# Expert stage: gated rows turned inside the next slot's first product, w2 split and y copies moved one step

## The reference, cut to what matters

```python
t = x.reshape(-1, D)                       # 1088 tokens, D = 1024
# top-1 group of 4, top-2 experts of its 4  ->  gates (1088, 16)
for e in range(16):                        # w1, w3: (1024, 256), w2: (256, 1024)
    he = jax.nn.silu(t @ w1[e]) * (t @ w3[e])
    y = y + gates[:, e:e + 1] * (he @ w2[e])
```

## Time and profile before

| | us |
|---|---|
| median of 3 timed runs | 1383.54 (1375.72 to 1384.65) |
| the profiled execution | 1374.35 |
| its span, first to last instruction | 1372.5 |
| mean granted TensorE clock | 0.91 of full |
| PE busy | 1166.7 (85%) |
| DVE busy | 710.0 (52%) |
| ACT busy | 505.1 (37%) |
| POOL busy | 312.5 (23%) |

### The profile page before, as it was taken

One profiled execution on the slowest core, in us unless ns is written; L12 is line 12 of the kernel. 1 busy time (PEld: TensorE's weight loads), 2 busy tenths in 40 slices (PEclk: granted clock), 3 DMA queues, 4 the chain that ended last, 5 costly groups with the idle time before them and its releaser, 6 DMA issues.

```text
span 1372.5 us, 17867 instructions
## 1 busy us (share of the span) xinstructions
PE 1166.7 (85%) x5729; PEld 897.7 (65%) x5729; DVE 710.0 (52%) x1310; ACT 505.1 (37%) x909; POOL 312.5 (23%) x273
## 2 busy tenths in 40 slices
PE   4999999898988989999899998963898988989920
PEld 3898799835757657575758585733676767767710
DVE  4320410255545445453546463425787878778737
ACT  3334122132112112121313131301777777777712
POOL 2101300000000000000000000001666656666646
PEclk9999999999696998878999999985999999999965
DMA  6340141270001101010101010003769786764278
GB/s 235 105 143 7 56 131 45 77 219 24 16 26 55 64 16 62 16 62 16 62 17 62 16 47 8 31 31 112 239 225 344 233 279 239 253 232 170 92 264 302
DMA packets 92946, 158.90 MB, mean 116 GB/s; under 512 B 12673, under 2 KB 61265, under 8 KB 92881
## 3 DMA queue, kind: packets, MB, share of 16 engines
q1 hardware_dynamic: 80112, 113.48, 24.5%
q0 software_dynamic: 11680, 42.47, 8.8%
q10 hardware_dynamic: 1088, 2.10, 0.4%
HBM read 167.80 MB, written 40.55 MB: 152 GB/s over the span
## 4 chain that ended last, share of the span: by engine, by line
PE 59%; DVE 10%; DMA 10%; issue 9%; ACT 7%; SPq 2%; POOL 2%; POOLq 1%; ACTq 0%; DVEq 0%
PE ps L896 9%; DMA below<-in_w 6%; PE ps L863 5%; PE ps L751 5%; PE ps L733 5%; DVE low L1564 3%; PE ps L1887 3%; PE ps L1889 3%; PE ps L1888 3%; PE ps L822 3%; PE ps L1882 2%; PE ps L1881 2%; PE ps L1883 2%; ACT high L1292 2%; SPq L1185 2%
## 5 line engine op out<-in xcount | busy, mean ns | idle before, releaser
L1564 DVE TENSOR_TENSOR low<-below,high 128x1024 fp32r<-128x1024 f32 x128 | 195.8, 1576 | 70.5 <-ACT high L1292 60.9
L1745 POOL TENSOR_SCALAR arena<-arena 128x1 f32<-128x1 f32 (+5 forms) x38 | 15.8, 417 | 747.6 <-ACT arena L691 366.9
L1253 POOL TENSOR_TENSOR low<-below,high 128x1024 fp32r<-128x1024 f32 x64 | 148.5, 2338 | 103.3 <-ACT high L1313 103.3
L1389 PE MATMUL ps<-high 128*128 128x512 f32 x384 | 156.0, 406 | 16.8 <-DVE low L1574 12.5
L538 ACT ACTIVATE arena<-ps 128x512 f32<-128x512 f32 (+7 forms) x109 | 56.9, 530 | 283.1 <-PE ps L733 282.8
L1391 PE MATMUL ps<-high,low 128*128 128x512 f32 x384 | 151.0, 393 | 0.0
L1390 PE MATMUL ps<-low,high 128*128 128x512 f32 x384 | 150.8, 393 | 0.0
L1292 ACT ACTIVATE high<-below 128x1024 fp32r<-128x1024 f32 x128 | 129.1, 1052 | 50.0 <-DMA below<-in_w 50.0
L896 PE MATMUL ps<-arena 128*128 128x512 f32 (+1 forms) x288 | 125.7, 594 | 2.9 <-ACT arena L538 2.4
L733 PE MATMUL ps<-arena 128*128 128x128 f32 (+4 forms) x613 | 104.3, 299 | 12.5 <-DVE arena L1093 4.8
L733 PEld LDWEIGHTS ps<-arena 128*128 128x128 f32 (+4 forms) x613 | 81.4, 165 | 31.2 <-issue 15.0
(11 more groups left out here) (214 smaller groups left out, 2036.2 us busy)
## 6 DMA issues: line engine op xcount, KB each, us to landing
below<-in_w SPq DMA_DIRECT2D x256, 256.0 KB
below<-in_w POOLq DMA_DIRECT2D x64, 512.0 KB
y_dram<-arena SPq DMA_DIRECT2D x32, 512.0 KB, 2.8
arena<-in_x_prompt SPq DMA_DIRECT2D x16, 512.0 KB
below<-in_w_in SPq DMA_DIRECT2D x12, 512.0 KB, 7.0
out<-arena SPq DMA_DIRECT2D x9, 512.0 KB, 5.3
arena<-in_w_o SPq DMA_DIRECT2D x1, 4096.0 KB, 16.5
h_dram<-arena SPq DMA_DIRECT2D x8, 512.0 KB, 2.6
```

Of the source, the lines that this page charges most:

```text
L1253: pool.tensor_tensor(w2_lo[s % UN][:, c], w2_in[:, c], w2_hi[s % UN][:, c].bitcast(F32), ALU.subtract).then_inc(s_w2lo, 1)
L1389: pe.matmul(out, x_hi, w_hi, start=start, stop=False)
L1564: dve.tensor_tensor(chunk(w13_lo[j], c), chunk(w13_in, c), chunk(w13_hi[j], c).bitcast(F32), ALU.subtract).then_inc(s_w13lo, 1)
```

## The change

PE: the two transposes of the gated rows of slot s-1 move from the end of body s-1 to the middle of the first product of slot s, before its fifth chunk (`gated_turn`). ACT and DVE take the high and low part there (`gated_high`, `gated_low`), between chunks of the next slot's w13 split, which is itself cut in pieces: chunks (0, 1) and (2, 3) on ACT, (0), (1, 2) and (3) on DVE, the last behind the gate product and the turned tokens. The y copies of slot s-2 stand at the start of body s. ACT casts w2 of slot s at the end of body s, where it cast that of slot s+1. POOL's low parts of w2 follow, and each w2 load is issued behind the split of its chunk.

ACT, one step in the steady part of the stage. Before: silu (L1327) of slot s, high parts of the turned tokens of s+1 (L1300), y copy of s-1 (L1305), g_hi of s (L1339), w2 of s+1 (L1313), w13 of s+2 (L1292).

The diff, cut to its core:

```diff
@@ -1235,25 +1235,26 @@
                 out=xg[:, s % UN, :], out_offset=None, in_=hn_dram,
                 in_offset=bass.IndirectOffsetOnAxis(ap=tok_i[:, s:s + 1], axis=0)).then_inc(s_xg[s % UN], 16)
 
-        def load_second(s):
-            e, new = expert(pool, s)
-            for c in range(2):
-                if s:
-                    pool.wait_ge(s_w2lo, 2 * s + c - 1)
-                pool.dma_start(w2_in[:, c], w2[0, bass.ds(e, 1), c * P:(c + 1) * P].rearrange("e p n -> p (e n)"),
-                               cond=new).then_inc(s_w2in[c], 16)
+        def load_second(s, c, e, new):
+            if s:
+                pool.wait_ge(s_w2lo, 2 * s + c - 1)
+            pool.dma_start(w2_in[:, c], w2[0, bass.ds(e, 1), c * P:(c + 1) * P].rearrange("e p n -> p (e n)"),
+                           cond=new).then_inc(s_w2in[c], 16)
 
         gather(0)
-        load_second(0)
+        e, new = expert(pool, 0)
+        for c in range(2):
+            load_second(0, c, e, new)
         gather(1)
         for s in range(SLOT_TILES):
-
+            if s + 1 < SLOT_TILES:
+                e, new = expert(pool, s + 1)
             for c in range(2):
                 pool.wait_ge(s_w2hi, 2 * s + c + 1)
                 pool.tensor_tensor(w2_lo[s % UN][:, c], w2_in[:, c], w2_hi[s % UN][:, c].bitcast(F32),
                                    ALU.subtract).then_inc(s_w2lo, 1)
-            if s + 1 < SLOT_TILES:
-                load_second(s + 1)
+                if s + 1 < SLOT_TILES:
+                    load_second(s + 1, c, e, new)
             if s + UN < SLOT_TILES:
                 gather(s + UN)
...
+        def gated_high(s):
+
+            act.wait_ge(s_mgt, s + 1)
+            if not is_zero(s):
+                act.wait_ge(s_my, s)
+            act.activation(g_hi, ps[:, 2, 0:2 * P].rearrange("p (a b) -> p a b", a=2),
+                           ACT.Copy).then_inc(s_mga, 1)
+
+        split_weights(0, 0, range(WC))
         turned(0)
-        split_second(0, 0)
 
         def body(it, j, first, last):
             s = it * UN + j
             start = first and j == 0
+            if not first:
+                free_y(act, it, j)
+                y_half(s - 2, j)
             if not last:
-                split_weights(s + 1, (j + 1) % UN)
+                split_weights(s + 1, (j + 1) % UN, (0, 1))
+            if not start:
+                gated_high(s - 1)
+            if not last:
+                split_weights(s + 1, (j + 1) % UN, (2, 3))
             act.wait_ge(s_mh, s + 1)
             if not start:
                 act.wait_ge(s_mg, s)
             act.activation(act_h, ps[:, 3 + j, 0:FF], ACT.Silu).then_inc(s_ms, 1)
             if not last:
                 turned(s + 1)
-            if not start:
-
-                if not first:
-                    free_y(act, it, j)
-                y_half(s - 1, (j - 1) % UN)
-
-            act.wait_ge(s_mgt, s + 1)
-            if not start:
-                act.wait_ge(s_my, s)
-            act.activation(g_hi, ps[:, 2, 0:2 * P].rearrange("p (a b) -> p a b", a=2),
-                           ACT.Copy).then_inc(s_mga, 1)
-            if not last:
-                split_second(s + 1, (j + 1) % UN)
+            split_second(s, j)
 
         expert_turns(act, body)
-        free_last(act)
-        y_half(SLOT_TILES - 1, (SLOT_TILES - 1) % UN)
+        for s in range(SLOT_TILES - 2, SLOT_TILES):
+            if s == SLOT_TILES - 1:
+                gated_high(s)
+            free_last(act, s)
+            y_half(s, s % UN)
...
+        def gated_turn(s):
+
+            pe.wait_ge(s_mg, s + 1)
+            if not is_zero(s):
+                pe.wait_ge(s_mga, s)
+                pe.wait_ge(s_mgv, s)
+            for c in range(2):
+                ins = pe.transpose(ps[:, 2, c * P:(c + 1) * P], g_row[:, c * P:(c + 1) * P], ident)
+            ins.then_inc(s_mgt, 1)
+
...
+                if kc == 4 and not start:
+                    gated_turn(s - 1)
                 if kc % 2 == 0:
                     pe.wait_ge(s_w13hi, WC * s + kc // 2 + 1)
                     pe.wait_ge(s_w13lo, WC * s + kc // 2 + 1)
@@ -1439,15 +1450,9 @@
                 turn(s + 1, it + (j + 1) // UN, (j + 1) % UN)
             if not start:
                 down(s - 1, (j - 1) % UN)
-            pe.wait_ge(s_mg, s + 1)
-            if not start:
-                pe.wait_ge(s_mga, s)
-                pe.wait_ge(s_mgv, s)
-            for c in range(2):
-                ins = pe.transpose(ps[:, 2, c * P:(c + 1) * P], g_row[:, c * P:(c + 1) * P], ident)
-            ins.then_inc(s_mgt, 1)
 
         expert_turns(pe, body)
+        gated_turn(SLOT_TILES - 1)
         down(SLOT_TILES - 1, (SLOT_TILES - 1) % UN)
...
+            if not first:
+                free_y(dve, it, j)
+                y_half(s - 2, j)
             if not last:
-                split_weights(s + 1, (j + 1) % UN)
+                split_weights(s + 1, (j + 1) % UN, (0,))
+            if not start:
+                gated_low(s - 1)
+            if not last:
+                split_weights(s + 1, (j + 1) % UN, (1, 2))
             dve.wait_ge(s_ms, s + 1)
             if not start:
                 dve.wait_ge(s_mgt, s)
             dve.tensor_tensor(g_row, act_h, ps[:, 3 + j, FF:2 * FF], ALU.mult).then_inc(s_mg, 1)
             if not last:
                 turned(s + 1)
-            if not start:
-                if not first:
-                    free_y(dve, it, j)
-                y_half(s - 1, (j - 1) % UN)
-
-            dve.wait_ge(s_mga, s + 1)
-            if not start:
-                dve.wait_ge(s_my, s)
-            dve.tensor_tensor(g_lo, ps[:, 2, 0:2 * P].rearrange("p (a b) -> p a b", a=2),
-                              g_hi.bitcast(F32),
-                              ALU.subtract).then_inc(s_mgv, 1)
+                split_weights(s + 1, (j + 1) % UN, (3,))
 
```

More of the change, by code:

```diff
@@ L1283, in moe_act, with split_weights @@
         act.activation(rt[:, 8, 0:45], rt[:, 8, 0:45], ACT.Exp).then_inc(s_rexp, 1)
-        def split_weights(s, j):
-            for c in range(WC):
+        def split_weights(s, j, chunks):
+            for c in chunks:
                 act.wait_ge(s_w13in[c], 32 * (s + 1))
@@ L1313, in split_second @@
                 act.activation(w2_hi[j][:, c], w2_in[:, c], ACT.Copy).then_inc(s_w2hi, 1)
-        split_weights(0, 0)
+        def gated_high(s):
[5 more added lines that the diff above has]
+        split_weights(0, 0, range(WC))
         turned(0)
-        split_second(0, 0)
         def body(it, j, first, last):
@@ L1356, in free_y, with free_last @@
     def free_y(eng, it, j):
[L1358 to L1369, removed]
+        if isinstance(it, int) and it < 2:
+            return
+        eng.wait_ge(s_yst[j], (it - 1) * 16)
+    def free_last(eng, s):
         eng.wait_ge(s_yst[s % UN], s // UN * 16)
@@ L1579, in y_half, with gated_low @@
             dve.tensor_copy(y_row[:, j, 512:1024], ps[:, 7, :]).then_inc(s_myv, 1)
-        split_weights(0, 0)
+        def gated_low(s):
+            dve.wait_ge(s_mga, s + 1)
+            if not is_zero(s):
+                dve.wait_ge(s_my, s)
+            dve.tensor_tensor(g_lo, ps[:, 2, 0:2 * P].rearrange("p (a b) -> p a b", a=2),
+                              g_hi.bitcast(F32), ALU.subtract).then_inc(s_mgv, 1)
+        split_weights(0, 0, range(WC))
         dve.wait_ge(s_mx, 1)
@@ L1595, in body @@
                 turned(s + 1)
-            if not start:
-                if not first:
-                    free_y(dve, it, j)
-                y_half(s - 1, (j - 1) % UN)
-            dve.wait_ge(s_mga, s + 1)
-            if not start:
-                dve.wait_ge(s_my, s)
-            dve.tensor_tensor(g_lo, ps[:, 2, 0:2 * P].rearrange("p (a b) -> p a b", a=2),
-                              g_hi.bitcast(F32),
-                              ALU.subtract).then_inc(s_mgv, 1)
-        expert_turns(dve, body)
-        free_last(dve)
-        y_half(SLOT_TILES - 1, (SLOT_TILES - 1) % UN)
+                split_weights(s + 1, (j + 1) % UN, (3,))
+        expert_turns(dve, body)
+        for s in range(SLOT_TILES - 2, SLOT_TILES):
+            if s == SLOT_TILES - 1:
+                gated_low(s)
+            free_last(dve, s)
+            y_half(s, s % UN)
         end_phase(dve, 2)
```

## The result

The changed kernel takes 1612.57 us, median of 4 runs (1605.25 to 1618.94), against 1383.30 us for the kernel before in the same comparison: a ratio of 1.167, interval 1.160 to 1.174. Forecast was 1574 in a range of 1531 to 1621. The profiled execution took 1605.25 us, with a span of 1603.5.

A forecast was written before the change was run, and what follows sets the result against it. The bound was taken to be a one-step chain through ACT's w2 cast, POOL's splits and the gather: 17.1 us against 10.8 over 30 steps, +189, plus 0.8 at the end, +190 on 1383.54 gives 1574 us, range 1531 to 1621.

The forecast's parts named there:

- (b): Late w2 cast on ACT delays POOL's splits and gather: one-step chain between token transposes (T), 17.1 us against 10.8, +189 us.
- the first link: From the start of PE's token transposes to ACT's first cast: 1.07 us at full clock, 1.97 at half.
- rival 1: PE falls to half clock in each step while waiting for the gather: step 18.0 us, 1600 us in all; chance 0.18.
- My check of the chain against that first slot: Kernel before, slot 0: token transposes to the issue of slot 2's gather took 10.2 us, against 10.5 in the forecast chain.
- the end behind T(31): After the last slot's token transposes start, w2 is cast behind silu: 18.8 us to the end against 18.1, +0.8 us.
- my term of 2.8 us: The twelve matmuls of the last second product, each about half of the 0.43 us one takes at half clock.
- (a): Gated turn between chunk products cuts the old loop: alone, steps of PE's 9.7 us, a gain of 1.1 us each.
- rival 3: Every gather lands in time and PE's 9.7 us bounds the step: 33 us less, 1351 us; chance 0.03.
- (c): POOL's w2 loads issued one after each split: no term beyond the gap already counted between the splits.
- (d): w13 split spread over ACT and DVE, chunk 3 freed last: waits for its reload hide in a 17 us step, nothing.
- Rival 2: The chain bounds but is short, splits not meeting DVE's and gathers landing in 5.1 us: 15.7 us a step, 1531; chance 0.12.
- The landing: From POOL's issue of the token gather to its data landing: median 6.5 us taken, 5.0 at least, 9.1 at most.

The follow-up runs named there:

- the run without loads: The change with POOL's gather issued ahead of its w2 splits, and weight loads of slots 1 to 31 left out: 1338.79 us, ratio 0.970 to the kernel before.
- the two pairs of runs with and without loads: Weight loads of slots 1 to 31 kept or left out: change with gather ahead of splits, 1381.99 and 1338.79 us; kernel before, 1383.30 and 1375.17 us.

## Why the prediction was right

**The chain (b).** Right in kind and in place; in size it is 1.05 us a step short. From the trace after, means over the 30 steps, with the forecast in brackets: T to ACT's first cast 1.88 us (1.07), to the w2 cast 0.97 (0.97), to POOL 1.14 (1.14), both splits and the gap 6.06 (4.99 + 1.1), second split to gather 1.40 (1.2), landing 6.47 (6.5), landing to T 0.21 (0.1). Sum 18.12 against 17.1.

**The term that was mis-sized** is the first link. I took the clock at full speed and gave the other case, rival 1, a chance of 0.18 and a time of 1600 us. Rival 1 is what happened, and the step of 18.12 lies outside the 16.3 to 17.7 to which I gave 0.63: the sign and the chain were foreseen, but that the time lies in the range I owe to a range wide enough for rival 1 as well. 26 of the 30 steps had the link at 1.98 or 2.01 us, one at 1.63, three at 1.07 to 1.10. PE fell to half clock at every one of the 29 waits for the gather (in three of them only 0.4 to 1.1 us behind T), and was at full clock again 3.1 to 6.0 us behind T, before the middle of the first product. This is 0.8 of the 1.0 us a step that the forecast lacked; the rest is 0.2 for the longer issue of the load before the gather, and 0.1 at the landing. The Trainium skill, TensorE: Matmul & The Clock Gate, section Loop structure matters more than you think, had this right, and I gave the one wait in the kernel's own first slot too little weight: it was the very wait that the change repeats 29 times. My check of the chain against that first slot, 10.2 us against 10.5, could not show the error: the 10.2 hold the link at half clock (0.9 us more than I took) and lack the wait and the load between the splits (1.1 us), so the two differences hid each other.

**The account of the whole.** The two spans differ by 1603.5 - 1372.5 = 231.0 us. The 30 steps are 543.63 - 323.86 = 219.8 of it (forecast 189), the end behind T(31) 4.8. Of these I had forecast 0.8 up to the last product; that product begins 21.0 us behind T(31), at 1541.7, where it was 17.7 before, with PE at half clock again in most of the last twelve matmuls. (By its own working my term of 2.8 us for these is 2.6, twelve halves of 0.43.) The remaining 6.4 lie ahead of T(1), nearly all in code that the change leaves alone: over the profiled executions of this study T(1) falls anywhere from 960.6 to 981.9 us, so I take them for a difference of the executions.

**The cut loop (a) and rival 3.** The idle time before the gated turn went to nothing, as forecast, and the run without loads shows the 9.7 us a step (9.44). What I had not seen is that this gain would not come even with the gather in time. "w2_in comes earlier than ACT wants it" in (c) and "Nothing" in (d) hold at 18 us a step, not at 10: there the weight loads cost 1.35 us a step, against 0.3 in the kernel before, and that takes back all of the 1.05 (shown by the two pairs of runs with and without loads).

**Rival 2** falls: splits did meet (2.8 us for the first one in every step), and a landing near 5.1 is only half of the case. The landings fall in two groups: 16 took 4.1 to 5.9 us, and 14 took 7.3 to 9.4. On the queue of SP's DMAs 1.1 to 1.4 MB moved beside each of the 14, and nothing beside the 16.

**The landing.** Over all gathers of the change:

```profile
DMA to landing us min/median/max: 4.1/5.8/9.4
```

The mean over the 30 steps is 6.5, what I took, but no single step is like it: the term stands for two kinds of step. In the kernel before the mean was 6.8 and the median 6.5, so the landings were a little shorter in the longer steps of the change; why, no run here isolates.

## What to carry to other kernels

An instruction that is moved delays more than what reads its result: it delays everything that is queued behind whatever waits for it, on every engine. Here a cast on ACT was moved to a place where its own consumer had ample time, and a gather on POOL that has nothing to do with it became the bound. Follow each moved instruction's semaphore to the queue that waits for it, and read that queue to its next DMA; count over how many steps the loop closes, and divide its length by that number. And keep prefetches ahead of the work in their queue that waits for this step's results.

## What was not expected of the hardware

PE's clock fell even at short waits. The same line in two steps of the change, and the matmuls behind it in the first:

```profile
1440.80 1.06 PE L1399 MATMUL ps<-arena 128*128 128x128 f32 x8 [2.75 <-DMA arena<-hn_dram,arena]
...
1442.78 0.63 PE L1388 MATMUL ps<-high 128*128 128x512 f32 x1
...
1472.77 1.94 PE L1399 MATMUL ps<-arena 128*128 128x128 f32 x8 [3.48 <-DMA arena<-hn_dram,arena]
```

After the wait of 3.48 us the eight transposes took 1.94 us, at half clock; before T(31) a wait of 3.13 us was enough for the same (1.97). After 2.75 us they took 1.06, still at full clock, but the matmuls right behind them took 0.63 instead of 0.39: the granted clock fell 1.1 us behind T. After a wait of 2.83 us, before T(16), it went the same way. In the step shown further up the matmuls took 0.40 us, the time at full clock, from 3.8 us behind T on.

In the steps that are written out in line (three at the start, one at the end), T came 0.04 us after the gather's landing; in those inside the loop with a counter, where the wait's value is in a register, 0.23 us in every one. That the register is the cause is not shown.

Two splits with both inputs in SBUF, one on DVE and one on POOL, hardly overlapped. In the change the one that began second took longer by what was left of the first, less at most 0.15 us, in 73 of 78 meetings; so DVE's 1.22 us split stretched POOL's from 2.0 to 2.8 us when it had begun 0.3 us earlier. In the other five DVE's had begun first, by 0.05 to 0.43 us, and yet was the one held up: it took 3.2 to 3.6 us, and POOL's 2.0.
